# Moving activation tiles to rows and bases at 64 modulo 256 bytes in a two-block float32 kernel

## The reference

```python
# first block, 16 meta tokens ahead of x (272 tokens in all)
proj  = rmsnorm(h, g1) @ w_in                      # u, q, k, v, two gates
mixed = sigmoid(g_ssm) * (s5_mixer(u) @ w_ssm_out) \
      + sigmoid(g_att) * (diff_attention(q, k, v) @ w_att_out)
h = h + mixed @ w_o                                # 1024 x 1024
hn = rmsnorm(h, g2)                                # feed-forward, D_FF = 2816
h = h + (gelu(causal_conv3(hn @ w_a)) * (hn @ w_b)) @ w_down
# second block, on the 256 tokens
z = rms_norm(x, norm_mix) @ w_in_2                 # 3072 columns
y = concat(rms_norm(rglru(z)), hgrn2(z), rms_norm(moba_attention(z)))
x = x + y @ w_out_2                                # 1024 x 1024
u = square(relu(rms_norm(x, norm_mlp) @ w_ff1))    # 4096 wide
x = x + u @ w_ff2
return rms_norm(x, norm_final)
```

## Time and profile before

| | us |
|---|---|
| median of 3 runs | 758.46 |
| lowest and highest | 755.24, 758.72 |
| the profiled execution | 755.43 |
| its span, first to last instruction | 753.7 |
| PE busy | 722.5 (96%) |
| DVE busy | 539.8 (72%) |
| ACT busy | 382.4 (51%) |

### The profile page before, as it was taken

The page is one execution under the profiler, slowest core; times in us unless marked ns, Lnnn a source line. Parts: engine busy times, 40 slices in busy tenths (PEclk is TensorE's granted clock), DMA queues, the critical chain, the costliest instruction groups (busy, mean ns, idle before and its releaser), DMA issues.

```text
span 753.7 us, 14566 instructions
## 1 busy us (share of the span) xinstructions
PE 722.5 (96%) x6150; PEld 675.7 (90%) x6150; DVE 539.8 (72%) x954; ACT 382.4 (51%) x565; POOL 29.7 (4%) x60
## 2 busy tenths in 40 slices
PE   6999999989989899999999999999889999999997
PEld 4988898888989899999999999888889988998995
DVE  6899985455778776776777798956868556556553
ACT  6477366366356334344433784488554343443441
POOL 6010000000000000000000240000000000000000
PEclk9999999999999999999999999999999999999999
DMA  8741133233545365555565544333335555565541
GB/s 238 205 160 59 57 116 109 60 112 112 168 157 180 113 201 190 170 199 191 173 205 183 186 158 154 126 111 114 104 121 196 168 196 195 170 199 191 173 163 56
DMA packets 94701, 115.67 MB, mean 153 GB/s; under 512 B 7971, under 2 KB 83932, under 8 KB 94636
## 3 DMA queue, kind: packets, MB, share of 16 engines
q1 hardware_dynamic: 94244, 114.51, 46.5%
q0 software_dynamic: 128, 0.13, 0.1%
q10 hardware_dynamic: 264, 0.10, 0.1%
HBM read 113.69 MB, written 1.05 MB: 152 GB/s over the span
## 4 chain that ended last, share of the span: by engine, by line
PE 72%; DVE 18%; ACT 5%; issue 3%; DMA 1%; SPq 0%; DVEq 0%; ACTq 0%
PE psum L1768 15%; PE psum L1769 15%; PE psum L1770 14%; DVE w_lo L1072 5%; PE psum L2293 4%; PE psum L2292 4%; PE psum L2291 4%; PE psum L2063 3%; PE psum L2059 3%; PE psum L2061 3%; ACT w_hi L503 2%; DVE sz L991 1%; PE psum L1911 1%; DMA xtok<-in_x_dram 1%; DVE b_prod L991 1%
## 5 line engine op out<-in xcount | busy, mean ns | idle before, releaser
L1072 DVE TENSOR_TENSOR w_lo<-w_raw,w_hi 128x2048 fp32r<-128x2048 f32 x105 | 240.1, 2289 | 99.9 <-ACT w_hi L503 99.7
L503 ACT ACTIVATE w_hi<-w_raw 128x2048 fp32r<-128x2048 f32 x105 | 199.6, 1906 | 59.1 <-PE psum L2293 41.5
L1768 PE MATMUL psum<-x2n_hi,w_hi 128*128 128x256 f32 x400 | 115.1, 288 | 2.0 <-DVE x2n_lo L1495 1.1
L1769 PE MATMUL psum<-x2n_lo,w_hi 128*128 128x256 f32 x400 | 112.8, 282 | 0.0
L1770 PE MATMUL psum<-x2n_hi,w_lo 128*128 128x256 f32 x400 | 112.6, 282 | 0.0
L1768 PE MATMUL psum<-hs_hi,w_hi 128*128 128x256 f32 (+1 forms) x352 | 100.2, 285 | 3.0 <-DVE ff L991 3.0
L1770 PE MATMUL psum<-hs_hi,w_lo 128*128 128x256 f32 (+1 forms) x352 | 100.0, 284 | 0.0
L1769 PE MATMUL psum<-hs_lo,w_hi 128*128 128x256 f32 (+1 forms) x352 | 99.9, 284 | 0.0
L1768 PEld LDWEIGHTS psum<-x2n_hi,w_hi 128*128 128x128 f32 x400 | 75.3, 188 | 5.2 <-DVE x2n_lo L1495 1.7
L1769 PEld LDWEIGHTS psum<-x2n_lo,w_hi 128*128 128x128 f32 x400 | 75.4, 189 | 0.7
L1770 PEld LDWEIGHTS psum<-x2n_hi,w_lo 128*128 128x128 f32 x400 | 75.4, 188 | 0.0
(11 more groups left out here) (444 smaller groups left out, 1544.5 us busy)
## 6 DMA issues: line engine op xcount, KB each, us to landing
w_raw<-in_w_ff_dram SPq DMA_DIRECT2D x32, 1024.0 KB, 5.2
w_raw<-in_w_in_dram SPq DMA_DIRECT2D x27, 1024.0 KB, 5.3
w_raw<-in_w_up_dram SPq DMA_DIRECT2D x22, 1024.0 KB, 5.1
w_raw<-in_w_down_dram SPq DMA_DIRECT2D x11, 1024.0 KB, 5.0
w_raw<-in_w_o_dram SPq DMA_DIRECT2D x4, 1024.0 KB, 5.1
w_raw<-in_w_out_dram SPq DMA_DIRECT2D x4, 1024.0 KB, 5.4
w_raw<-in_w_ssm_out_dram SPq DMA_DIRECT2D x2, 1024.0 KB, 5.2
w_raw<-in_w_att_out_dram SPq DMA_DIRECT2D x2, 1024.0 KB, 5.1
```

The costliest lines, as they stand in the source:

```text
L503: A.activation(w_hi[:, u % NW, :], raw[:, u % NRAW, :], ACT.Copy).then_inc(sem("hi_ready"), 1)
L1072: V.tensor_tensor(w_lo[:, u % NRAW, :], raw[:, u % NRAW, :], w_hi[:, u % NW, :].bitcast(F32), ALU.subtract).then_inc(sem("lo_ready"), 1)
L1768: T.matmul(out_, lh, rh, start=start, stop=False)
L1769: T.matmul(out_, lh, rl, start=False, stop=False)
```

## The change

It gives other addresses to the tiles of the second block, to the mixer outputs (mix_hi, mix_lo) and to the inputs of the first feed-forward part (hs_hi, hs_lo). The order of instructions, waits and DMAs on every engine stays as it is.

- All tiles of the second block and its feed-forward part move up by 64 bytes: x2n, ycat, relu, uu, u_hi, u_lo, and the small tiles of its mixers. Their bases go from 0 to 64 modulo 256, and with rows of 1,024 bytes (or 512) all their rows with them.
- mix_hi and mix_lo get rows of 320 numbers, 1,280 bytes or 5 x 256, of which the first 258 are used, and bases at 64 modulo 256.
- hs_hi and hs_lo get rows of 1,280 bytes with a base at 0 modulo 256, and are used from column T0 = 14 on. So a row as up_a reads it begins at 56, as up_b reads it at 64.

```diff
+ROW = 320
...
-        mix_hi = sb("mix_hi", [P, KD, NQ], F32R, k(0))
-        mix_lo = sb("mix_lo", [P, KD, NQ], F32R, k(8704))
+        mix_hi = sb("mix_hi", [P, KD, ROW], F32R, k(30080))
+        mix_lo = sb("mix_lo", [P, KD, ROW], F32R, k(40320))
...
-        hs_hi = sb("hs_hi", [P, KD, NQ], F32R, k(98304))
-        hs_lo = sb("hs_lo", [P, KD, NQ], F32R, k(106560))
+        hs_hi = sb("hs_hi", [P, KD, ROW], F32R, k(88128))[:, :, T0:TOK]
+        hs_lo = sb("hs_lo", [P, KD, ROW], F32R, k(98368))[:, :, T0:TOK]
...
-        x2n_hi = sb("x2n_hi", [P, KD, 256], F32R, k(0))
-        x2n_lo = sb("x2n_lo", [P, KD, 256], F32R, k(8704))
+        x2n_hi = sb("x2n_hi", [P, KD, 256], F32R, k(64))
+        x2n_lo = sb("x2n_lo", [P, KD, 256], F32R, k(8768))
...
-        ycat_hi = sb("ycat_hi", [P, KD, 256], F32R, k(33856))
-        ycat_lo = sb("ycat_lo", [P, KD, 256], F32R, k(42048))
+        ycat_hi = sb("ycat_hi", [P, KD, 256], F32R, k(33920))
+        ycat_lo = sb("ycat_lo", [P, KD, 256], F32R, k(42112))
...
-        relu = sb("relu", [P, 2, 2, 256], F32, k(50240))
-        uu = sb("uu", [P, 2, 2, 256], F32, k(54336))
-        u_hi = sb("u_hi", [P, 2, 2, 256], F32R, k(58432))
-        u_lo = sb("u_lo", [P, 2, 2, 256], F32R, k(62528))
+        relu = sb("relu", [P, 2, 2, 256], F32, k(50304))
+        uu = sb("uu", [P, 2, 2, 256], F32, k(54400))
+        u_hi = sb("u_hi", [P, 2, 2, 256], F32R, k(58496))
+        u_lo = sb("u_lo", [P, 2, 2, 256], F32R, k(62592))
...
-                A.activation(mix_hi[:, m, :], gate[:, m, :], ACT.Copy, scale=0.5).then_inc(sem("mix_hi"), 1)
+                A.activation(mix_hi[:, m, 0:NQ], gate[:, m, :], ACT.Copy, scale=0.5).then_inc(sem("mix_hi"), 1)
```

More of the change, by code:

```diff
@@ L290, in program @@
-        rst1 = sb("rst1", [P, 258], F32, k(112704))
-        lru_w = sb("lru_w", [P, 2, 2, P], F32, k(109632))
-        rst3 = sb("rst3", [P, 256], F32, k(111680))
-        relu = sb("relu", [P, 2, 2, 256], F32, k(50240))
-        uu = sb("uu", [P, 2, 2, 256], F32, k(54336))
-        u_hi = sb("u_hi", [P, 2, 2, 256], F32R, k(58432))
-        u_lo = sb("u_lo", [P, 2, 2, 256], F32R, k(62528))
-        outb = sb("outb", [P, 2, D], F32, k(66624))
-        nf = sb("nf", [P, D], F32, k(74816))
-        sqj = sb("sqj", [P, 2, 512], F32, k(78912))
+        ycat_hi = sb("ycat_hi", [P, KD, 256], F32R, k(33920))
@@ new lines, in program @@
+        ycat_lo = sb("ycat_lo", [P, KD, 256], F32R, k(42112))
+        xc = sb("xc", [P, 2, 256], F32, k(50304))
+        lru_r = sb("lru_r", [P, 2, 256], F32, k(52352))
+        lru_i = sb("lru_i", [P, 2, 256], F32, k(54400))
+        lru_a = sb("lru_a", [P, 2, 256], F32, k(56448))
+        lru_t = sb("lru_t", [P, 2, 256], F32, k(58496))
+        lru_g = sb("lru_g", [P, 2, 256], F32, k(60544))
+        hgq = sb("hgq", [P, 2, 256], F32, k(62592))
+        hgk = sb("hgk", [P, 2, 256], F32, k(64640))
@@ new lines, in program @@
+        hgf = sb("hgf", [P, 2, 256], F32, k(66688))
+        hqf = sb("hqf", [P, 2, 256], F32, k(68736))
+        htot = sb("htot", [P, 512], F32, k(70784))
+        hA = sb("hA", [P, 8, P], F32, k(72832))
+        hX = sb("hX", [P, 4, P], F32, k(76928))
+        hgo = sb("hgo", [P, 2, 256], F32, k(78976))
+        cq = sb("cq", [P, 4, 256], F32, k(81024))
+        ck = sb("ck", [P, 4, 256], F32, k(85120))
+        cv = sb("cv", [P, 2, 512], F32, k(89216))
+        mp = sb("mp", [P, 2, 384], F32, k(93312))
@@ new lines, in program @@
+        mpT = [sb(f"mpT{i}", [P, 2, 384], F32, k((96384, 45184)[i])) for i in range(2)]
+        mo = sb("mo", [P, 4, 256], F32, k(99456))
+        sq2 = sb("sq2", [P, 2, 256], F32, k(103552))
+        sq3 = sb("sq3", [P, 2, 256], F32, k(107648))
+        rst2 = sb("rst2", [P, 256], F32, k(105600))
+        rsm2 = sb("rsm2", [4, 256], F32, k(106624))
+        sqs = sb("sqs", [P, 8, 256], F32, k(89216))
+        rst1 = sb("rst1", [P, 258], F32, k(112768))
+        lru_w = sb("lru_w", [P, 2, 2, P], F32, k(109696))
@@ L301, in program @@
+        rst3 = sb("rst3", [P, 256], F32, k(111744))
+        relu = sb("relu", [P, 2, 2, 256], F32, k(50304))
+        uu = sb("uu", [P, 2, 2, 256], F32, k(54400))
+        u_hi = sb("u_hi", [P, 2, 2, 256], F32R, k(58496))
+        u_lo = sb("u_lo", [P, 2, 2, 256], F32R, k(62592))
+        outb = sb("outb", [P, 2, D], F32, k(66688))
+        nf = sb("nf", [P, D], F32, k(74880))
+        sqj = sb("sqj", [P, 2, 512], F32, k(78976))
         psum = ctx.enter_context(nc.psum_tensor("psum", [P, 8, 512], F32))
@@ L1404, in mix_low @@
                 dve.wait_ge(sem("mix_hi"), j + 1)
-                V.scalar_tensor_tensor(out=mix_lo[:, j, :], in0=gate[:, j, :], scalar=0.5,
-                                       in1=mix_hi[:, j, :].bitcast(F32), op0=ALU.mult,
+                V.scalar_tensor_tensor(out=mix_lo[:, j, 0:NQ], in0=gate[:, j, :], scalar=0.5,
+                                       in1=mix_hi[:, j, 0:NQ].bitcast(F32), op0=ALU.mult,
                                        op1=ALU.subtract).then_inc(sem("mix_lo"), 1)
```

## The result

The changed kernel takes 751.7 us in the median of six runs (749.18 to 754.78), the kernel before 757.8 us beside it. The ratio is 0.9932, with a 95% interval of 0.9910 to 0.9954: shorter by 3.5 to 6.8 us. The forecast was 742.5 us, 16.0 us under the median that it started from. The direction was right; the measured gain, 6.1 us, is less than half of that.

The account below looks back on a forecast made before the run. The prediction took PE to bound the kernel, busy 96% of the span. Its eight terms summed to 14.0 us, taking 755.43 to 741.4 us; allowing for the median it forecast 742.5 us, range 734 to 757.

Parts of the forecast that it names:

- Term 3: up_a, first feed-forward: 528 matmuls 5.0 ns faster, 2.6 us, from a range of 0 to 2.6.
- Term 4: w_o, on the mixer outputs: 192 matmuls 6.0 ns faster, 1.2 us.
- Term 2: up_b, first feed-forward: 528 matmuls 5.25 ns faster, 2.8 us.
- Term 1: ff1, second feed-forward: 768 matmuls 4.75 ns faster, 3.6 us, all on the path.
- Terms 5 and 6: Second block's input projection: 1.0 us from nine units with activations moving, 0.2 us from three token-major units with activations stationary.
- Term 7: w_out2: 192 matmuls 4.75 ns faster, partly lost to waits on DVE; 0 to 0.9 us, taken as 0.45.
- Term 8: ff2, second feed-forward: 384 matmuls of 512 columns, stationary tile moved; 0 to 4.5 us, taken as 2.2.
- The first rival: Whole kernel: no effect, 755 to 758 us, ff's pace coming from its block's structure; chance 0.20.
- The second rival: Only moving rows at exactly 64 gain; up_a, ff2 and token units gain nothing: 747.3 us, chance 0.16.
- The third: Slower, 768 us: the distance between moving and weight row counts, and 64 is the bad one; chance 0.08.

Follow-up runs that it names:

- e11: The changed kernel run once more, unaltered: 749.94 us, ratio 0.9928 to the kernel before.
- e6: Weight buffers 64 bytes further, at 192 modulo 256, activations unmoved: 760.28 us on the kernel before, 758.91 us on the changed kernel.
- e12: The changed kernel with a 16-column matmul ahead of up_b in steps 2 and 6 and of ff1 in steps 3 and 8: 749.99 us, ratio 0.9927.
- e13b: The changed kernel with a 16-column matmul ahead of up_b in step 6 and ahead of ff1 in step 8: 748.86 us.

## Why the prediction was right and wrong

The mechanism was half right. That PE sets the time, that start to start is the pace, that DVE and ACT don't care about the addresses, that the supply keeps up: all held. That rows at 64 would run at ff's pace held for ff1 (5.47 us against 5.46 forecast), though not in every execution.

**The step that failed** is the premise under the sum, "if every moved row gets ff's 7.1 ns", with "down unchanged" beside it. It took a pace that ff showed at 256 columns for a property of the address. The runs showed three things in its place: the blocks of 258 columns stay at 119.8 and 120.8 ns (terms 3 and 4, 3.8 us that never came); a 256-column block at that distance has two paces, and up_b ran at the slow one in the profile (term 2, 0.6 us instead of 2.8); and a slow up_b takes down with it, a loss of 2.2 us that stood in no term. By terms, in the profile, with the loop blocks counted from the tables above:

- Term 1, ff1, 3.6 us: 0.22 us in each of the 14 steps behind the first ff2, and 0.2 in the two units ahead of it, 3.3 us. In an execution such as e11 it is only 0.5.
- Term 2, up_b, 2.8 us: 0.05 x 11 = 0.6 in the profile; 2.7 in the executions where the loop is fast. The size was right for one of two patterns, and the prediction did not know of two.
- Term 3, up_a, 2.6 us: nothing (5.75 us against 5.74). The argument was that 256 of its 258 columns lie where up_b's lie. The lower end, nothing, was in the range for the wrong reason: the width decides, not the start.
- Term 4, w_o, 1.2 us: nothing, for the same reason. It had no lower end in the sum, and should have had one: its 258 columns had no row at ff's pace behind them.
- Terms 5 and 6, the second projection, 1.2 us: 1.4, of which the token-major units gave 0.1.
- Term 7, w_out2, 0.45: nothing. Its groups of 24 became 0.1 us shorter (the first from its first start to its last, 2.73 to 2.61 us), but PE waited that much longer between them: from the first of its matmuls to the next block it was 29.13 us before and 29.16 after. The 0.22 us of that stretch come from the first units of ff1. The lower end of the range was the right one.
- Term 8, ff2, 2.2 us: 0.08 x 15 = 1.2, between its ends.
- Not in the sum: down. "With down unchanged at 5.46" was wrong by 0.2 us in each of 11 blocks, 2.2 us lost.

In the best case, both loops fast, the stretches of the first loop and the last one take 160.88 us (e11) and 170.28 (the changed kernel) instead of 163.06 and 174.57; with the 1.4 and 0.2 us between, the gain is 8.1 us for a like opening. The other 5.9 of the 14.0 were never there: chiefly terms 3 and 4 (3.8 us) and 1.0 of term 8. Where the first loop is slow it is 4.0 us less.

Small slips in the working changed nothing. A step of the first feed-forward by the forecast's own blocks is 5.50 + 5.46 + 5.46 = 16.4 us, not 16.1, and needs 193 GB/s, not 196. The low end of the range by its own sum is 735.3 us, not 734. The measured 751.7 us lies in the range only because that reached up into the rival without an effect.

The first rival (no effect) is refuted by the result and by e6: the same activations, the weights moved, and the gain gone. By the rule of the Trainium skill ("TensorE: Matmul & The Clock Gate", Part 2, Step-by-step: what each phase is for) loading the next weights takes no read bandwidth from the running matmul. The measurement decides: ff goes from 113.7 to 118.5 ns in e6 with only the weights moved by 64 bytes. Whether it is read bandwidth that is lost, no run shows. The second rival, a gain of 8.1 us, came nearest to the measured 6.1, and named the wrong reason: it had up_b gain in full and ff2 not at all. The third named the right quantity, the distance, and had its effect the wrong way round: with the moving row 64 bytes short of the weight row (192) 256 columns run best, 64 bytes past it they do not (117.7 ns). ff's row alone could not tell address from distance; xn's rows 1 and 5, which spoke against the forecast, were of 272 columns, and no such width was seen at the fast pace.

The scatter that every total here has comes in good part from elsewhere. The opening, whose order of instructions is the same in all of these kernels, took 214.5 to 219.4 us in the profiles. It goes with the number of stretches in which the clock was granted at half. In e12's (219.07 us) the clock was at half between 166 and 170 us and again between 194 and 197 us, in e13b's (214.90 us) in neither; the stretch behind 85 us was in both. Over all profiles the opening took 214.5 to 214.9 us with none of the later stretches, 215.5 to 216.8 with one and 217.7 to 219.4 with two. A pattern worth 4.0 us in the first loop of some executions is hard to see in medians of six runs beside that. That the patterns come from reads of the two operands that meet is argued, not shown: no run shows such a meeting itself, only its cost by distance, width and history. Why 258 columns never settle was not tried further, nor any width between 258 and 272, nor ff2 at distance 0.

## What to carry to other kernels

Where PE bounds, read its pace from start to start, block by block, and compare it with columns over clock: blocks of the same shape that differ by 5 ns a matmul may differ in how their operands lie. Look at the distance between the moving and the stationary row, not at one address, and test it with the width that the block really has. When two executions of the same code differ, look whether a loop has fallen into different patterns; the pace of an untouched block is part of what a change of its neighbour can cost. And give a stage's saving to the time only after its waits are read: w_out2 got faster, and waited longer.

## What the runs showed of the hardware

- At full clock settled blocks of 256-column matmuls have paces from 113.3 to 119.8 ns, by the distance between their operands modulo 256 bytes, and the 258 columns of up_a and w_o about 120 ns wherever they started. At half clock hs started every 0.21 us, which is its 258 columns at 1.2 GHz with nothing added.
- At distance 192 the stream has two self-repeating patterns, 113.3 and 117.8 ns. It carries the one it is in across blocks, and across a 258-column block. A 16-column matmul put in between led from the slow to the fast one in six of six cases at full clock, and costs 0.35 us.
- One program fell into different patterns in different executions, worth 0.39 us of a 17 us step in the first loop and 0.21 us of an 11 us step in the second.
